# A merged schedule of attention, convolution and recurrence steps: each spread step is placed behind the eviction that directly follows a weight unit

## What is computed

```python
def second_block(x, mem, ...):
    for l in range(2):
        h = rms_norm_2(x, ng[0])
        x = x + 0.5 * rms_norm_2(swiglu(h, ffn_w1[l, 0], ffn_w3[l, 0], ffn_w2[l, 0]), ng[1])
        y = mixer_block(rms_norm_2(x, ng[2]), ...)
        x = x + rms_norm_2(y, ng[3])
        y = cross_attention(rms_norm_2(x, ng[4]), rms_norm_2(mem, mem_norm[l]), ...)
        x = x + rms_norm_2(y, ng[5])
        x = x + 0.5 * rms_norm_2(swiglu(rms_norm_2(x, ng[6]), ...), ng[7])

def mixer_block(h, ...):
    u_conv, q, k, v, u_pool, gates = split(h @ w_in)
    y_conv = conv_branch(u_conv, ...)            # GLU, a 31-tap causal convolution, layer norm, product
    y_attn = diff_attention(q, k, v, ...) @ attn_o   # 8 heads, two softmaxes a head
    y_pool = pool_branch(u_pool, ...)            # windowed means, four group products, product
    return (g0 * y_conv + g1 * y_attn + g2 * y_pool) @ w_out
```

## Time and profile before

| what | us |
|---|---|
| three runs | 2380.88, 2382.08, 2392.05 (median 2382.08) |
| the profiled execution, whole | 2374.37 |
| the profiled execution, span of the trace | 2372.6 |
| PE busy in the span | 2253.6 (95%) |
| DVE busy in the span | 1709.4 (72%) |
| ACT busy in the span | 1180.0 (50%) |

### The profile page before, as it was taken

The page is one execution under the profiler, slowest core; times in us unless marked ns, Lnnn a source line. Parts: engine busy times, 40 slices in busy tenths (PEclk is TensorE's granted clock), DMA queues, the critical chain, the costliest instruction groups (busy, mean ns, idle before and its releaser), DMA issues.

```text
span 2372.6 us, 43783 instructions
## 1 busy us (share of the span) xinstructions
PE 2253.6 (95%) x17949; PEld 2155.6 (91%) x17949; DVE 1709.4 (72%) x2733; ACT 1180.0 (50%) x1843; POOL 91.6 (4%) x86
## 2 busy tenths in 40 slices
PE   6998998999999999989899999999999989999998
PEld 5976898999999997789898999999998789898998
DVE  6766886896665798787655764775797787665764
ACT  2565445774544533555544544544533455544543
POOL 1000000110010000000000010010000000000110
PEclk7998999999999999899999999999999899999999
DMA  8634575667565663345553766566663345463754
GB/s 237 200 116 134 163 239 170 193 191 246 164 203 185 199 185 107 106 136 178 161 178 107 209 192 194 170 204 188 191 180 104 116 134 179 141 193 102 222 175 137
DMA packets 399911, 405.11 MB, mean 171 GB/s; under 512 B 18182, under 2 KB 392312, under 8 KB 399713
## 3 DMA queue, kind: packets, MB, share of 16 engines
q1 hardware_dynamic: 396177, 389.27, 54.1%
q0 software_dynamic: 3536, 13.04, 1.8%
HBM read 401.17 MB, written 1.09 MB: 170 GB/s over the span
## 4 chain that ended last, share of the span: by engine, by line
PE 71%; DVE 19%; ACT 5%; issue 4%; DMA 1%; DVEq 0%; POOL 0%; ACTq 0%; POOLq 0%
PE gemm_ps L952 46%; PE gemm_ps L955 15%; DVE weights_lo L1582 6%; DVE x_res L2048 4%; PE misc_ps L1093 2%; PE misc_ps L1094 2%; ACT weights_hi L1209 1%; DVE mod_partial L1681 1%; ACT e L1376 1%; DVE h_lo L1720 1%; PE misc_ps L1126 1%; PE misc_ps L1090 1%; PE misc_ps L1111 1%; DVE neg_max L1808 1%; DVE y L1756 1%
## 5 line engine op out<-in xcount | busy, mean ns | idle before, releaser
L1582 DVE TENSOR_TENSOR weights_lo<-raw_weights,weights_hi 128x1024 fp32r<-128x1024 f32 x704 | 836.6, 1200 | 374.9 <-ACT weights_hi L1209 371.4
L1209 ACT CAST weights_hi<-raw_weights 128x1024 fp32r<-128x1024 f32 x704 | 716.8, 1032 | 623.9 <-PE gemm_ps L952 432.8
L952 PE MATMUL gemm_ps<-h_hi,weights_hi 128*128 128x256 f32 x3280 | 930.3, 284 | 20.0 <-DVE h_lo L1710 8.5
L952 PE MATMUL gemm_ps<-h_lo,weights_hi 128*128 128x256 f32 x3280 | 915.5, 279 | 0.0
L952 PE MATMUL gemm_ps<-h_hi,weights_lo 128*128 128x256 f32 x3280 | 915.2, 279 | 0.0
L952 PEld LDWEIGHTS gemm_ps<-h_hi,weights_hi 128*128 128x128 f32 x3280 | 622.6, 190 | 27.7 <-issue 22.0
L952 PEld LDWEIGHTS gemm_ps<-h_lo,weights_hi 128*128 128x128 f32 x3280 | 622.9, 190 | 3.1 <-issue 2.7
L952 PEld LDWEIGHTS gemm_ps<-h_hi,weights_lo 128*128 128x128 f32 x3280 | 621.5, 189 | 0.0
L2048 DVE SCALAR_TENSOR_TENSOR x_res<-zp,param_cols,x_res 128x256 f32<-128x256 f32 x480 | 197.0, 483 | 0.0
L955 PE MATMUL gemm_ps<-weights_lo,hidh 128*128 128x256 f32 x688 | 190.2, 276 | 0.0
L955 PE MATMUL gemm_ps<-weights_hi,hidh 128*128 128x256 f32 x688 | 190.2, 276 | 0.0
(11 more groups left out here) (326 smaller groups left out, 3136.2 us busy)
## 6 DMA issues: line engine op xcount, KB each, us to landing
raw_weights<-in_ffn_w_dram SPq DMA_DIRECT2D x256, 512.0 KB, 4.3
raw_weights<-in_w_in_dram SPq DMA_DIRECT2D x200, 512.0 KB, 4.0
raw_weights<-in_w_mod_dram SPq DMA_DIRECT2D x48, 512.0 KB, 5.0
raw_weights<-in_w_up_dram SPq DMA_DIRECT2D x44, 512.0 KB, 4.6
raw_weights<-in_xattn_kv_dram SPq DMA_DIRECT2D x32, 512.0 KB, 4.4
raw_weights<-in_w_out_dram SPq DMA_DIRECT2D x24, 512.0 KB, 4.4
raw_weights<-in_w_down_dram SPq DMA_DIRECT2D x20, 512.0 KB, 4.7
raw_weights<-in_w_branch_dram SPq DMA_DIRECT2D x16, 512.0 KB, 4.4
```

What stands on the lines that cost most here:

```text
L952: mm = pe.matmul(ps[:, c, 0:T], w[:, m, kt, c * P:(c + 1) * P], x[:, f, :], start=start, stop=stop_)
L1209: act.copy(unit_of(WH, m % SPLIT, u), unit_of(RAWB, u["raw"] % RAW, u)).then_inc(sems["weights_rounded"], 1)
L1582: dve.tensor_tensor(unit_of(WL, m % SPLIT, u), unit_of(RAWB, u["raw"] % RAW, u), unit_of(WH, m % SPLIT, u), ALU.subtract).then_inc(sems["w ...
```

## The change

`spread` looks at the step behind each unit. If it is an eviction, the slots due after this unit are not put between the two; they are put right behind the eviction. Nothing else differs, and the number of slots due is counted as before.

```diff
@@ -156,13 +156,14 @@
 
         n = sum(kind == "unit" for kind, _ in main)
         out, seen, put = [], 0, 0
-        for step in main:
+        for i, step in enumerate(main):
             out.append(step)
-            if step[0] == "unit":
-                seen += 1
-                while put < len(slots) * seen // n:
-                    out += slots[put]
-                    put += 1
+            seen += step[0] == "unit"
+            if step[0] == "unit" and i + 1 < len(main) and main[i + 1][0][:4] == "evac":
+                continue
+            while put < len(slots) * seen // n:
+                out += slots[put]
+                put += 1
         return out
 
     def collect(fn):
```

## The result

The changed kernel took 2388.20 us (median of 20 executions, 2377.78 to 2402.99), the kernel before 2381.14 (20 executions). The ratio is 1.0032, 95% interval 1.0018 to 1.0047, so the change costs about 7.6 us (4.3 to 11.2). The forecast was 2381.8, no change. The profiled execution of the changed kernel has a span of 2390.2, 17.6 more than before. That is more than the 7.6 because the profiled execution before (2374.37) is the fastest of its 20, and the changed kernel's (2392.03) is 3.8 over its median.

A forecast was written before the change was run, and what follows sets the result against it. PE, busy 95% of the span, was taken as the bound, with DVE full in places. Block 1 -2.0 and -1.3, mixers 2 x (3.1 - 1.3), sum +0.3 us faster: 2381.8, range 2370 to 2392.

The follow-up runs named there:

- e9: New order behind evictions in mixers and cross attentions only, evac_branch left in place, against the kernel before: 2381.54 us, ratio 1.0017.
- e4: New order only for evac_scaled and evac_pool_w, block 1 unchanged, against the kernel before: 2377.85 us, ratio 0.9988.
- e6: Kernel before with 5 to 16 matmuls of constants put at places where PE waits, against the kernel before: 2392.62 us, ratio 1.0048.
- e12: e4 plus 16 matmuls of constants in the wait ahead of each mixer's last-head transposes, against the kernel before: 2368.08 us, ratio 0.9963.
- e2: New order in mixers and cross attention only, block 1 in the old order, against the kernel before: 2389.08 us, ratio 1.0032.
- e10: e4 plus evac_branch directly behind its unit in the mixers, against the kernel before: 2378.58 us, ratio 1.0004.
- e13: e9 plus 4 matmuls of constants ahead of the first two heads' scores in each mixer, against the kernel before: 2378.04 us, ratio 0.9991.
- e11: Changed kernel with PE waits filled by matmuls of constants, except where the filling itself waited for a slot, against the kernel before: 2382.13 us, ratio 1.0017.
- e14: e12 with PE's waits in block 1 filled by matmuls of constants too, against the kernel before: 2368.19 us, ratio 0.995.

## What to carry over

Putting evictions right behind their producer makes strictly ordered engines wait for that producer. It cost where nobody waited for the slot (e9); where PE did wait for it (e4) the gain is within the interval. Take each wait by its length and by what the tensor engine's clock does behind it: at the pool products the same 5 us of idle time went with 3.4 or with 20.5 us at half the clock. Work of constants put into a wait that can't be removed is worth trying, but its own waits must be long over (e6 against e12). And before a gain seen in one trace is put down to a change, look for it in traces without the change.

## What the runs showed of the chip that I had not expected

- A wait of 0.85 us ahead of the scores in e9 was followed by half the clock, and one of 0.55 us in its second layer. The wait of 2.86 us ahead of the first statistic in the kernel before wasn't (nor in e2 and e4), but in e9, e10, e12 and e13 the same 2.86 us were. What decides it stays open.
- The same order falls into one of two patterns of the clock in block 1, with the old order and with the new; with the old order PE gets 2.6 to 5.6 us later from 110 to 262 in the one, and no later in the other. The Trainium skill (TensorE: Matmul & The Clock Gate, "What's actually happening") says that how many matmuls run at the low clock at a kernel's start varies from run to run of one and the same kernel. These traces show such a variation in the middle of a kernel. What decides between the two patterns stays open.
- 1.05 us of matmuls of constants in the wait ahead of the scores went with full clock there, in both layers of e13; 16 or 17 of them in the wait at the last head kept it up in all six instances of e11, e12 and e14, where it fell in all 20 without.
